# An encoder layer on eight cores: the first layer norm of half the tokens behind the output projection, its f32 result kept, GpSimd without arithmetic in the MLP, and h squared on ScalarE

## What is computed

```python
proj = x @ w_in                              # gates b, c, value (512 each), pool input (512)
y_conv = gate_b * short_conv(gate_c * value)  # 3 taps along the sequence
y_pool = multiscale_pool(pool_in)             # windows 2, 4, 8, 16, then a 128x128 map per group
mix = concat(y_conv, y_pool) @ w_out
x1 = layer_norm(ALPHA * x + mix, ln1_g, ln1_b)
h = square(relu(x1 @ w_ff1))
y = layer_norm(ALPHA * x1 + h @ w_ff2, ln2_g, ln2_b)
```

## Time and profile before

| | us |
|---|---|
| median of 6 runs | 1221.06 |
| lowest, highest | 1217.10, 1336.08 |
| profiled execution: its time | 1218.37 |
| its span, first to last instruction of the slowest core (core 4) | 1216.8 |
| busy in the span: PE, DVE, ACT, POOL | 1140.6, 969.3, 325.1, 478.1 |

### The profile page before, as it was taken

One profiled execution on the slowest core, in us unless ns is written; L12 is line 12 of the kernel. 1 busy time (PEld: TensorE's weight loads), 2 busy tenths in 40 slices (PEclk: granted clock), 3 DMA queues, 4 the chain that ended last, 5 costly groups with the idle time before them and its releaser, 6 DMA issues.

```text
span 1216.8 us, 17092 instructions; the slowest of 8 cores (1206.1 to 1216.8 us)
## 1 busy us (share of the span) xinstructions
PE 1140.6 (94%) x5313; PEld 517.4 (43%) x5313; DVE 969.3 (80%) x1242; ACT 325.1 (27%) x611; POOL 478.1 (39%) x330
## 2 busy tenths in 40 slices
...
GB/s 153 196 114 183 215 170 153 194 247 115 156 250 190 174 140 171 133 189 165 173 150 137 180 206 174 158 218 104 192 198 147 139 158 189 201 145 138 161 133 70
DMA packets 111034, 203.14 MB, mean 167 GB/s; under 512 B 38624, under 2 KB 71520, under 8 KB 108000
## 3 DMA queue, kind: packets, MB, share of 16 engines
...
HBM read 149.73 MB, written 75.50 MB: 185 GB/s over the span
## 4 chain that ended last, share of the span: by engine, by line
PE 77%; DVE 9%; DMA 7%; issue 5%; ACT 1%; POOL 1%; DVEq 0%; SPq 0%; ACTq 0%; POOLq 0%
PE bank L735 54%; PE bank L331 23%; DMA scr_h<-hst_94 2%; DMA scr_z<-ring_83 1%; DMA win<-w_in 1%; DMA ring_87<-scr_z 1%; DMA x1T_90<-scr_xb 1%; DVE w_55 L342 1%; DMA x1T_89<-scr_xb 1%; DMA ring_83<-xe 1%; DVE st L559 1%; DVE hS_110 L342 1%; DVE w_56 L342 0%; DVE nmr L338 0%; DVE z_100 L342 0%
## 5 line engine op out<-in xcount | busy, mean ns | idle before, releaser
L335 ACT ACTIVATE sd<-mv 128x1 f32<-128x1 f32 x64 | 12.9, 201 | 418.1 <-DVE mv L561 402.6
L331 PE MATMUL bank<-xT_64,win 128*128 128x512 bf16 (+1 forms) x608 | 113.5, 346 | 1.9 <-DMA win<-w_in 1.2
L331 PE MATMUL bank<-xT_65,win 128*128 128x512 bf16 x512 | 111.5, 379 | 0.0
L331 PEld LDWEIGHTS bank<-xT_64,win 128*128 128x128 bf16 x608 | 59.0, 98 | 55.6 <-issue 3.8
L331 PEld LDWEIGHTS bank<-xT_65,win 128*128 128x128 bf16 x512 | 50.0, 98 | 60.0
L335 ACT ACTIVATE bank<-bank 128x512 f32<-128x512 f32 x80 | 46.6, 582 | 95.1 <-PE bank L735 93.9
L342 POOL TENSOR_TENSOR hst_94<-rt_102 128x512 bf16<-128x512 f32 x22 | 28.2, 1282 | 87.7 <-ACT rt_102 L335 87.7
L342 POOL TENSOR_TENSOR hst_95<-rt_101 128x512 bf16<-128x512 f32 x21 | 28.6, 1364 | 82.0 <-ACT rt_101 L335 82.0
L331 PE MATMUL bank<-wout,ycat_81 128*128 128x512 bf16 x256 | 56.1, 379 | 0.4 <-DVE ycat_82 L342 0.4
L331 PE MATMUL bank<-wout,ycat_82 128*128 128x512 bf16 x256 | 56.1, 379 | 0.1
L342 POOL TENSOR_TENSOR hst_96<-rt_103 128x512 bf16<-128x512 f32 x21 | 25.8, 1227 | 75.0 <-ACT rt_103 L335 75.0
...
## 6 DMA issues: line engine op xcount, KB each, us to landing
hr_108<-scr_h SPq DMA_DIRECT2D x8, 2048.0 KB, 9.7
hr_109<-scr_h SPq DMA_DIRECT2D x8, 2048.0 KB, 10.0
scr_h<-hst_94 SPq DMA_DIRECT2D x22, 512.0 KB, 3.5
scr_h<-hst_95 SPq DMA_DIRECT2D x21, 512.0 KB, 3.7
scr_h<-hst_96 SPq DMA_DIRECT2D x21, 512.0 KB, 3.6
ring_87<-scr_z SPq DMA_DIRECT2D x13, 512.0 KB, 7.1
ring_86<-scr_z SPq DMA_DIRECT2D x12, 512.0 KB, 6.0
ring_83<-xe SPq DMA_DIRECT2D x8, 512.0 KB, 10.4
```

What stands on the lines that cost most here:

```text
L331: pe.emit(lambda h: h.matmul(bank[bi][:, 0:cols], lhsT=lhsT, rhs=rhs, start=start, stop=stop), reads=reads, writes=[B_bank[bi]], signal=si ...
L335: act.emit(lambda h: h.activation(out=out, in_=in_, func=func, **kw), reads=reads, writes=writes, excl=excl)
```

## The change

- Ring of 8 buffers; tile i uses a fixed set of four (`XR`), so that two tiles in turn never share one.
- `wo` no longer stores all z. For 14 row blocks (`DIRECT`: three each of tiles 0 and 1, two each of tiles 2 to 5) the `ln1_pieces` run on the ring buffer right behind `evac`. Of the other 18, which still go through `scr_z`, four (`RELOAD`) are loaded back in stage 1, one beside each of tiles 2 to 5, and 14 (`LK`) in ff1. `pop` takes 3 pieces at four places of a tile in place of 2 at five.
- `fin` writes f32 in place; SP stores it to a new DRAM tensor `scr_x1`, and POOL's queue stores it with a cast to bf16 to `scr_xb`. `nmr` and `xbs` are gone.
- ff2 loads `scr_x1` as its residual rows; `resid` is gone, with its ScalarE and GpSimd operations.
- `relu_sq` squares with a second ScalarE activation instead of GpSimd.
- The transposing loads `tr` are issued two blocks after the last block norm that they need. `load_h` is split into four DMAs; the first unit's four are issued in blocks 2, 5, 8 and 11 of the last pair instead of all in block 0; gamma and beta of the second norm are loaded in block 0 of that pair.

```diff
@@ ring and layer-norm pieces
+        XR = ((0, 1, 2, 5), (3, 4, 6, 7))
...
             def center():
                 ln_rstd(p, rs, B_rstd[i][s])
                 a_stt(v, v, mv[:, 0:1], gam1, ALU.subtract, ALU.mult, [B_mv[i][s], B_g1], Bv)
-                a_stt(nm, mv[:, 0:1], -1.0, rs, ALU.mult, ALU.mult, [B_mv[i][s], B_rstd[i][s]], [B_nmr[i][s]])
 
             def fin():
-                a_stt(xb, v, rs, bet1, ALU.mult, ALU.add, [B_rstd[i][s], B_b1] + list(Bv), [B_xb])
-                load(sp, scr_xb[i, 128 * s:128 * s + 128, :], xb, S_xb[xq], [B_xb], [B_scb[i][s]])
+                a_stt(v, v, rs, bet1, ALU.mult, ALU.add, [B_rstd[i][s], B_b1], Bv)
+                load(sp, scr_x1[i, s], v, S_rs[r], Bv, [B_sc1[i][s]])
+                load(pool, scr_xb[i, 128 * s:128 * s + 128, :], v, S_cs[r], Bv, [B_scb[i][s]])
+        DIRECT = {(i, s) for i in range(6) for s in range(3 if i < 2 else 2)}
+        RELOAD = {2: (0, 3), 3: (1, 3), 4: (2, 2), 5: (2, 3)}
@@ def wo
                     evac(b[2 * t:2 * t + 2], r)
-                    load(sp, scr_z[i, s], ring[r], S_rs[r], B_ring[r], [B_scz[i][s]])
+                    if (i, s) in DIRECT:
+                        pieces.extend(ln1_pieces(i, s, r))
+                    else:
+                        load(sp, scr_z[i, s], ring[r], S_rs[r], B_ring[r], [B_scz[i][s]])
@@ loop of stage 1
-            wo(i, i + 1, ld + [lambda: pop(2)],
-               end=[lambda i=i: (W1[i - 2].sums() if i >= 2 else None, pop(2))])
+            wo(i, i + 1, ld + [lambda: pop(3)],
+               end=[lambda i=i: (W1[i - 2].sums() if i >= 2 else None, pop(3))])
+            def first(i=i):
+                pop(3)
+                if i in RELOAD:
+                    r = XR[i % 2][3]
+                    load_z(*RELOAD[i], r)
+                    pieces.extend(ln1_pieces(*RELOAD[i], r))
...
+            proj(i + 2, [first, xr, third, fourth])
@@ before ff1
+        LK = [(i, s) for i in range(2, NT) for s in range(NS) if (i, s) not in DIRECT and (i, s) not in RELOAD.values()]
+        LSLOT = (5, 3, 4, 6)
@@ relu_sq
             a_act(rt[r][0], src, AF.Relu, reads, [rt[r][1]], excl=excl)
             v = rt[r][0].rearrange("p (s t) -> p s t", t=128)
-            a_tt(pool, h_out(n, half, t), v, v, ALU.mult, [rt[r][1]], [B_hst[n % 3][2 * half + t]])
+            a_act(h_out(n, half, t), v, AF.Square, [rt[r][1]], [B_hst[n % 3][2 * half + t]])
@@ layer norm in ff1, loads
-            load(sp, zs[r], scr_z[i, s], S_zl[r], [B_scz[i][s]], B_zs[r])
+            load(sp, zs[r], scr_x1[i, s], S_zl[r], [B_sc1[i][s]], B_zs[r])
-        def resid(m, t):
...
+        LN_SLOT = [(n, h_) for n in range(1, NP * NQ) for h_ in (0, 1) if h_ == 0 or (n > 10 and n % 4 == 1)]
...
+        tr_at = {max(fin_at.get((i, NS - 1), 0) + 2, NQ * (i // 2 - 1) + 2): i for i in range(2, NT)}
@@ last pair of ff1
                 if q == 0:
-                    load_h(0)
                     W2[0].load()
+                    load(sp, gam2, g2_d, S_g2, [], [B_g2])
+                    load(sp, bet2, b2_d, S_b2, [], [B_b2])
                     for t in range(2):
                         load_zs(0, t)
+                if q in (2, 5, 8, 11):
+                    load_h(0, (q - 2) // 3)
```

More of the change, by code:

```diff
@@ L27 @@
 N_CORES = 8
-NRING = 6
+NRING = 8
 KB = 1024
@@ L260, in build_program @@
         rt = [tile(f"rt{q}", (172 + 2 * q) * KB, [512]) for q in range(3)]
-        xbs = [tile(f"xbs{q}", (190 + 2 * q) * KB, [D], BF16) for q in range(2)]
         gam1, B_g1 = tile("gam1", 194 * KB, [D])
@@ L291, in build_program @@
         B_scz = [[Buf(f"scz{i}_{s}") for s in range(NS)] for i in range(NT)]
+        B_sc1 = [[Buf(f"sc1{i}_{s}") for s in range(NS)] for i in range(NT)]
         B_scb = [[Buf(f"scb{i}_{s}") for s in range(NS)] for i in range(NT)]
@@ L296, in build_program @@
         B_rstd = [[Buf(f"rstd{i}_{s}") for s in range(NS)] for i in range(NT)]
-        B_nmr = [[Buf(f"nmr{i}_{s}") for s in range(NS)] for i in range(NT)]
         B_mv2 = [Buf(f"mv2{i}") for i in range(4)]
@@ L701, in fourth @@
                     W1[i].load()
-            proj(i + 2, [ln_hook, xr, third, fourth])
+            proj(i + 2, [first, xr, third, fourth])
         pop(len(pieces))
-        load_xr(NT - 1, 0, 4)
-        load_xr(NT - 1, 3, 3)
+        for s in range(NS):
+            load_xr(NT - 1, s)
         def xs1(q):
@@ L720, in xs4, with ln_load @@
                  [S_t["S4"][1]])
-        wo(NT - 2, NT - 1, mid=[lambda: (load_xr(NT - 1, 1, 0), load_xr(NT - 1, 2, 5))] +
-           [lambda c=c: W1[c].load() for c in range(5, 8)], end=[W1[4].sums])
-        wo(NT - 1, mid=[lambda: (xs1(0), xs2(0), xs3(0), xs4(0), W1[5].sums(), W1[8].load(), W1[9].load())])
+        LK = [(i, s) for i in range(2, NT) for s in range(NS) if (i, s) not in DIRECT and (i, s) not in RELOAD.values()]
+        LSLOT = (5, 3, 4, 6)
+        def ln_load(k):
+            load_z(*LK[k], LSLOT[k % 4])
+        wo(NT - 2, NT - 1, mid=[lambda c=c: W1[c].load() for c in range(5, 8)], end=[W1[4].sums])
+        wo(NT - 1, mid=[lambda: (xs1(0), xs2(0), xs3(0), xs4(0), W1[5].sums(), W1[8].load(), W1[9].load(), ln_load(0))],
+           end=[lambda: (ln_load(1), ln_load(2))])
         PROD = {"P1": ("X", "B11", "A11"), "P2": ("X", "B21", "A12"), "P3": ("Z", "B22", "S4"), "P4": ("Y", "T4", "A22"),
@@ L788, in ff1_back_b @@
             relu_sq(n, 0, 1, bank[b["Y"]][:], [], [B_bank[b["Y"]]])
-        zb_slot = {}
-        def load_zb(i, s, r):
-            load(sp, ring[r], scr_z[i, s], S_rl[r], [B_scz[i][s]], B_ring[r])
         def hx(q):
```

133 lines of the change are left out of this document (47 added, 86 removed).

## The result

The changed kernel takes 1183.11 us in the median of 10 runs (1180.03 to 1295.16), the kernel before, run beside it, 1219.89 (20 runs). The ratio is 0.9703, 95% interval 0.9684 to 0.9722: faster by 3.0%, or 36 us, where 47 were forecast. In some executions, the longest of these ten among them, the cores of one die show a lower granted clock and take longer; they are in the medians but not in the ratio. The profiled execution of the changed kernel took 1185.52 us; its slowest core is core 2, span 1184.0 (the other seven 1173.7 to 1178.9).

The account below looks back on a forecast made before the run. TensorE's idle time was to fall, most of it caused by VectorE, overloaded in the first pair and slowed beside GpSimd. 1218.4 - 59.2 (five ff1 and ff2 stages) + 12 (stage 1) = 1171 us, range 1148 to 1200.

Parts of the forecast that it names:

- ff2 units: The 14 ff2 units behind the first: 14.6 us lost would fall to 0.7; bounds 0.3 and 4.
- Rival 2: In ff2 the waits stay, being the round trip from P7 over VectorE to P4; 1185 us, chance 0.05.
- Pairs 2 and 3: Middle pairs of ff1: with transposing loads issued earlier, 9.9 us lost would fall to 3; bounds 1 and 7.
- the last pair: Last pair of ff1: shorter store-of-h stop and faster sums cut the loss from 14.4 to 7 us; bounds 4 and 12.
- First ff2 unit: Start of ff2: weight sums at 1.81 us each cut the loss from 9.9 to 0.9 us; bounds 0 and 3.
- Stage 1: Tiles 2 to 5: gates late behind a reloaded block's statistics, 3 us per tile, 12 in all; from nothing to 32.
- The first pair: First pair of ff1: loss falls from 34.0 to 12 us, 9 of it for a late first reload; bounds 4 and 20.
- VectorE's list: First pair of ff1: VectorE's work sets the pace, 6.1 us per block against 6.04, losing 1 us in all.
- the added transfers: Copies to `scr_x1` add 2 MB of DMA traffic; costed at nothing.
- rivals 3 and 4: ff1: ScalarE's Squares become the bound, 1204 to 1245 us (chance 0.04); Square and Sqrt swap tables, 1198 or 1234 (0.03).
- Rival 1: Stage 1 pays nothing because the reload lands before VectorE asks; 1159 us, chance 0.13.
- rival 5: Reload chains in stage 1 and at the start of ff1 stay as slow as before; 1199 us, chance 0.05.

Follow-up runs that it names:

- e7: Changed kernel with the old residual's ScalarE and GpSimd operations put back into each ff2 unit, on two buffers nobody reads; ratio 0.9818, 25.05 us per unit.
- e1: Changed kernel with the reload of stage 1 issued on SP's queue ahead of fin's store instead of behind it; ratio 0.9684.
- e6: Kernel before with only the square of h moved from GpSimd to ScalarE; ratio 0.9920.
- e2: Changed kernel with the layer-norm steps of ff1 starting at block 3 instead of block 1; ratio 0.9741.
- e9: Changed kernel with the transposing load of tile 2 issued in block 7 of ff1 instead of block 2; ratio 0.9699.
- e10: Changed kernel with tile 2's transposing load in block 7 of ff1 and the layer-norm steps from block 3 on, together; ratio 0.9722.

## Why the prediction was right, and where it was off

The range held (1148 to 1200), the sign and most stages too. By its steps:

- **ff2 units** (0.7 forecast, 0.0 measured) and the ground for it, fin and hs1 slowed beside GpSimd: right, and e7 shows the cause alone. I had called it a slowing; by the rows of e7 it is a wait for the other engine's operation to end. Rival 2, the waits staying as a round trip, is out.
- **Pairs 2 and 3** (3, 1.1) and **the last pair** (7, 7.9): inside their bounds. On core 2 the stop behind a store of h fell from 6.2 to 3.4 us (from matmul to matmul) but did not go: that store took 16.77 against 20.24, with the DMA share at 0.96 in that pair.
- **First ff2 unit** (0.9, 2.7): the weight sums took 1.81 each as forecast. What I had left out is TensorE at half its clock: TensorE stops 3.2 us at the end of ff1, and the first ten matmuls of the unit come 0.43 us apart instead of 0.2158.
- **Stage 1** (12, 14.7 on core 2, 13.5 in the median): the step was right in place and size. In tiles 2 to 5 the stops, from matmul to matmul, sum to 3.1 + 3.3 + 2.2 + 2.7 = 11.3, behind a reload that was issued after the fin's store; data forecast for 275 on the time axis of before came at 284.5 on one that lies 10 to 11 later. By e1 some 6 of these are the wait itself. What I had not priced is 4.8 at tile 0, where three block norms stand ahead of the gates with no reload at all, with center and fin at 2.0 and 1.9 beside the pooling sums. The norms alone do not make it: tile 1 has the same three, as long, and no stop. There VectorE comes to its first gate 5.8 us after the projection begins, at tile 0 10.9, having waited 2.9 us for a pooling sum on GpSimd before it emptied the banks of `wo(0)`.
- **The first pair** is the step that failed in size: a wait of 5.5, taken as 9 with the half clock, 2 for the backlog and 1 for VectorE's list, 12 in place of 34.0; measured 21.7 (20.0 in the median), at or beyond its upper bound of 20; the stage took 116.7 us, so the sign named for it, under 110, failed. The wait is the one named, at the place named. But I took the durations of the store and the load from the trace of before, 16.9 and 6.6; they were 19.7 and 10.3, and VectorE stood 12.7 instead of 5.5. A second reload (3.7) and stores of h (2.3 to 4.1 each) were late as well. What I take to stand behind it is an item that I had costed at nothing, the added transfers. I looked at the DMA share of whole stages, 0.77 before; in the 80 us that matter it is 1.05 to 1.11, and 0.74 to 1.03 in the kernel before.
- **What sets the pace of the first pair**: I had VectorE's list. e6, e2, e9 and e10 point to the transfers: neither the square alone, nor starting the norms later, nor freeing SP's list brings the pair under 18.6. That the sheer amount of data is the bound is argued from the DMA share; no run took transfers away to show it, and none gave the waiting stores more buffers.
- **The square** at 0.63 with no table load: right, and rivals 3 and 4 are out. The Trainium skill (ScalarE: Activation LUTs, Table sets: the hidden batching unit) says that a function outside the loaded set needs a load and does not name Square among those of every set; here 128 of them stand between the Sqrts with a single load in the whole trace.
- **The cast stores on POOL's list** "hold GpSimd until fin", costed at nothing: on that list the weight loads are what counts. They waited for the last cast store (343.2) and then ran ahead.

Rival 1 (stage 1 pays nothing) is out by 13.5 us; rival 5, slow chains, is the one that came half true: 8 to 10 us in the first pair, nearly nothing more in stage 1.
